# Layers run in halves of the tokens, per-token sums as single columns, x loaded first

## The chip, the cores and the metric

One core of a Trainium2 chip runs the whole program in one launch. The time is the device time of that launch in microseconds (us). Before the change it is 2333.32 us, the median of 3 runs (2330.7 to 2334.06). The profiled execution took 2335.25 us; its records cover a span of 2333.5 us. Engines are named as in the profile: PE is the matrix engine (PEld its loads of the stationary operand), DVE the vector engine, ACT the scalar engine, POOL GpSimd, SP the engine that issues most loads. An operand written 128x1024 has 128 partitions and 1024 elements in each.

## What is computed

`x` is 1024 tokens by 1024 features, float32. First come two layers of this form (`l` = 0, 1):

```python
shift, scale, gate = jnp.split(c_act @ w_ada[l] + b_ada[l], 3, axis=-1)
h = rms_norm(x, g_pre[l]) * (1.0 + scale) + shift
proj = h @ w_in[l]                       # 1024 -> 3072
y_a = b_a * causal_conv(c_a * u_a) * silu(gate_a)
y_p = causal_pool(u_p, ...) * silu(gate_p)
y = concatenate([y_a, y_p]) @ w_out[l]   # 1024 -> 1024
x = x + gate * rms_norm(y, g_post[l])
```

Then one hybrid layer:

```python
h = x @ w_in_2          # gmlp, two attentions, an index projection
mix = concatenate([gmlp(...), diff_attention(...), topk_attention(...)])
x = layer_norm(alpha * x + mix @ w_out_2, ln1_g, ln1_b)
gate, up = split(x @ w_gu_2)             # 2 x 2816
x = layer_norm(alpha * x + (silu(gate) * up) @ w_down_2, ln2_g, ln2_b)
```

Every norm needs, for each token, a sum over all 1024 features of its row. So the next product cannot begin for a token before the last product has ended for that token; for other tokens it could.

## The kernel before

**Layout.** Features lie on the partitions, in KT = 8 blocks `k` of 128, and the 1024 tokens lie along the free axis, as two halves of 512. A bank pair in PSUM (`bank[0..3]`, the name `pair` in the trace) holds 128 features of all 1024 tokens. A product of one *unit* makes one such block of 128 output features from all 1024 input features. Each float32 operand is split in two parts, `w_hi`/`w_lo` and `act_hi`/`act_lo`, and for each `k` three products are summed (hi·hi, hi·lo, lo·hi), each for both halves: 8 x 3 x 2 = 48 matmuls of 128x512 for a unit (`product`, L1565).

**Weights.** Units follow each other in two slots. For each unit SP loads 512 KB into `w_raw` (L446), ACT rounds it to `w_hi` (`hi_next`, L674), DVE makes `w_lo` (`lo_next`, L1022), and PE uses both. `w_hi` of a unit waits until PE has done with the unit two before it (`unit_done`), and the load waits for `lo_ready` of the unit before it in its slot.

**Order.** No scheduler is at work: each engine runs its instructions in the written order, and semaphores with constant or loop-counted values make it wait. What stands behind a waiting instruction in a queue waits too.

**Start.** SP loads the small parameters, then all of `x` as one transfer of 4 MB, then 16 pieces of `w_ada` (scale and shift of layer 0) four at a time. PE turns `x` into `xT` (L1487), DVE copies (L948) and sums the pieces weighted by `c` (L956, L958), `columns` (L1501) adds them over the partitions by matmuls against one column of ones.

**Per-token sums.** The squares of `x` or `y` (ACT L641, L720) are summed over the 8 blocks, for `y` on POOL (L573, L576), and over the partitions by `feature_sums` (L1494): a matmul with the square 128x128 `ones` as the stationary operand and 512 tokens moving, so that every partition gets all sums. DVE picks the diagonal (L965), reduces it to a column `rstd_col` (L967), scales and inverts it (L968, L969), ACT takes the root (L649), DVE makes a diagonal matrix of it (L973) and PE spreads it over the partitions again (L1508).

**A layer's end.** When all 8 units of the out projection are done, DVE scales `yT` (L1121) and adds it to `xT` for even `k` (L1127), POOL adds it for odd `k` (L581). Layer 1 then needs the sums of squares of the new `x`, and scales it: DVE L1032, ACT `act_hi` L683, DVE `act_lo` L1036. `product_two` (L1543, L1551) runs the first two units together, the parts with `act_hi` first, as they become ready `k` by `k`.

**The hybrid layer.** `act_hi` (L734) of the new `x`, two index units and one smaller, then 8 chunks of the value product (L1647) with 20 rounds of index scores (L1667 on PE, L764 on ACT, L1161/L1163 on DVE) between their steps, one every 3 steps; unit 0 and 1, 8 more chunks (L1647 again), units 2 to 13 (L1683), beside which the top-k threshold is found bit by bit; then attention in 48 items (L1735, L1749, L1767). Its output is scaled (L1387), turned (L1806) and multiplied by `w_out_2` (8 units, sum `z` L1398). The layer norm has a mean by matmul (L1820, L1827), centring (L1407), squares (ACT L888, POOL L625), their sum (L1494), root and spread as above, the scaling (L1416), `act_lo` (L1425) and the start of the second sum (L1431). The FFN's 22 hidden blocks go in groups of 6, 6, 6 and 4: gate and up units, `f_buf` (L1442), `f_hi` (L906), `f_lo` (L1444), then 8 units of the down product with partial sums on DVE (L1451). A second layer norm ends it: ACT shift (L919), PE turns (L1861), copies (L924, L1471), stores.

## Time and profile before

| what | value |
| --- | --- |
| median of 3 runs | 2333.32 us |
| profiled execution, its own time | 2335.25 us |
| span of its records | 2333.5 us |
| PE busy | 2168.3 us, 93% |
| DVE busy | 1038.1 us, 44% |
| ACT busy | 723.7 us, 31% |
| POOL busy | 168.8 us, 7% |
| mean granted clock of PE | 0.961 |

A share of busy time is an average. PE is near full for most of the span and has its idle time at a few places: the start, the two ends of layers, the way out of attention, the two layer norms. The rows that show them stand two sections below. The mean granted clock is 1 at PE's full rate and 0.5 at its lower one.

### The profile page before, as it was taken

How to read it: one execution, taken by the hardware profiler on the slowest of the kernel's cores; microseconds unless marked ns; L12 is line 12 of the kernel's file. 1: busy time of each engine (PE TensorE's matmuls, PEld its weight loads, DVE VectorE, ACT ScalarE, POOL GpSimd, SP SyncE). 2: the span in 40 equal slices, each digit the busy share in tenths (PEclk: the TensorE clock that was granted, in tenths of full speed). 3: DMA queues.
4: the chain of work that ended last, by engine and by line, in shares of the span. 5: the costliest groups of instructions: out<-in, count | busy, mean ns of one | idle time of the engine just before them, and what ended most of it. 6: DMA issues, size and time to landing. Idle time of an engine off the chain costs nothing.

```text
span 2333.5 us, 25535 instructions
## 1 busy us (share of the span) xinstructions
PE 2168.3 (93%) x9718; PEld 1698.4 (73%) x9718; DVE 1038.1 (44%) x1521; ACT 723.7 (31%) x1042; POOL 168.8 (7%) x132
## 2 busy tenths in 40 slices
PE   4899999889999988999988998979999999999995
PEld 3688887568888756688855667748888888888872
DVE  5744452453233235867778862262222222222235
ACT  2222123232212334555765552133211111111114
POOL 0000001200000121021200000210000000000021
PEclk9899999899999989999979999979999999999997
DMA  6423331101111104101100002101111112112101
GB/s 230 127 88 116 100 99 45 36 23 50 45 45 45 46 18 147 46 20 28 55 28 1 1 1 91 46 8 54 45 54 46 48 41 59 49 40 59 36 27 72
DMA packets 177131, 129.37 MB, mean 55 GB/s; under 512 B 5653, under 2 KB 167590, under 8 KB 176806
## 3 DMA queue, kind: packets, MB, share of 16 engines
q1 hardware_dynamic: 172454, 111.67, 15.6%
q0 software_dynamic: 4608, 16.78, 2.1%
q8 instruction: 44, 0.72, 0.1%
q14 instruction: 25, 0.20, 0.0%
HBM read 120.04 MB, written 8.39 MB: 55 GB/s over the span
## 4 chain that ended last, share of the span: by engine, by line
PE 83%; DVE 9%; ACT 4%; issue 1%; DMA 1%; POOL 0%; SPq 0%; DVEq 0%; ACTq 0%; PEldq 0%
PE pair L1565 59%; PE pair L1543 5%; PE pair L1683 4%; PE pair L1647 4%; PE pair L1767 2%; PE pair L1551 2%; PE pair L1735 1%; PE pair L1494 1%; DVE act_region L1310 1%; PE pair L1749 1%; DVE yT L1121 1%; PE pair L1667 1%; PE pair L1508 1%; ACT proj L785 1%; DVE xT L1127 1%
## 5 line engine op out<-in xcount | busy, mean ns | idle before, releaser
L1022 DVE TENSOR_TENSOR w_lo<-w_raw,w_hi 128x1024 fp32r<-128x1024 f32 x147 | 180.2, 1226 | 995.5 <-ACT w_hi L674 995.4
L1565 PE MATMUL pair<-act_hi,w_hi 128*128 128x512 f32 x1680 | 518.3, 390 | 4.0 <-DVE w_lo L1022 2.4
L1565 PE MATMUL pair<-act_lo,w_hi 128*128 128x512 f32 x1680 | 517.3, 389 | 0.0
L1565 PE MATMUL pair<-act_hi,w_lo 128*128 128x512 f32 x1680 | 517.2, 389 | 0.0
L674 ACT ACTIVATE w_hi<-w_raw 128x1024 fp32r<-128x1024 f32 x148 | 157.0, 1061 | 1010.2 <-PE pair L1565 954.3
L1565 PEld LDWEIGHTS pair<-act_hi,w_hi 128*128 128x128 f32 x1680 | 314.4, 188 | 73.1 <-issue 8.5
L1565 PEld LDWEIGHTS pair<-act_lo,w_hi 128*128 128x128 f32 x1680 | 315.3, 188 | 65.7
L1565 PEld LDWEIGHTS pair<-act_hi,w_lo 128*128 128x128 f32 x1680 | 315.3, 188 | 65.5
L1565 PE MATMUL pair<-f_hi,w_hi 128*128 128x512 f32 x352 | 108.5, 389 | 2.2 <-DVE f_lo L1444 2.2
L1565 PE MATMUL pair<-f_lo,w_hi 128*128 128x512 f32 x352 | 108.4, 389 | 0.0
L1565 PE MATMUL pair<-f_hi,w_lo 128*128 128x512 f32 x352 | 108.4, 389 | 0.0
L1543 PE MATMUL pair<-act_hi,w_hi 128*128 128x512 f32 x224 | 78.4, 434 | 24.6 <-ACT act_hi L734 10.4
L1767 PEld LDWEIGHTS pair<-proj,act_region 128*128 128x128 f32 x576 | 73.8, 202 | 34.5 <-issue 18.7
L1767 PE MATMUL pair<-proj,act_region 128*128 128x128 f32 (+1 forms) x576 | 82.7, 292 | 2.1 <-ACT act_region L845 2.1
L1735 PE MATMUL pair<-proj 64*128 64x512 f32 (+3 forms) x288 | 72.0, 582 | 8.9 <-DVE neg_max L1310 5.8
L835 ACT ACTIVATE act_region<-act_region,neg_max 128x128 f32<-128x128 f32 (+7 forms) x96 | 73.4, 768 | 16.9 <-DVE neg_max L1310 16.7
L1565 PEld LDWEIGHTS pair<-f_hi,w_hi 128*128 128x128 f32 x352 | 66.0, 188 | 16.2 <-issue 2.6
L1543 PEld LDWEIGHTS pair<-act_hi,w_hi 128*128 128x128 f32 x224 | 44.3, 209 | 44.4 <-issue 18.0
L1565 PEld LDWEIGHTS pair<-f_hi,w_lo 128*128 128x128 f32 x352 | 66.1, 188 | 13.7
L1565 PEld LDWEIGHTS pair<-f_lo,w_hi 128*128 128x128 f32 x352 | 66.1, 188 | 13.7
L1543 PE MATMUL pair<-act_hi,w_lo 128*128 128x512 f32 x224 | 75.7, 422 | 0.0
L615 POOL COPY sum<-z 128x1024 f32<-128x1024 f32 x2 | 2.1, 1039 | 962.6 <-DVE z L1451 704.5
(306 smaller groups left out, 2706.5 us busy)
## 6 DMA issues: line engine op xcount, KB each, us to landing
w_raw<-w_in SPq DMA_DIRECT2D x64, 512.0 KB, 3.8
w_raw<-w_gu SPq DMA_DIRECT2D x44, 512.0 KB, 3.8
w_raw<-w_out SPq DMA_DIRECT2D x24, 512.0 KB, 4.1
w_raw<-w_down SPq DMA_DIRECT2D x24, 384.0 KB, 3.4
sq<-w_ada POOLq DMA_DIRECT2D x16, 512.0 KB, 3.6
sq_sum<-w_ada POOLq DMA_DIRECT2D x16, 512.0 KB, 4.6
yT<-x SPq DMA_DIRECT2D x1, 4096.0 KB, 14.5
x_mid<-xT SPq DMA_DIRECT2D x1, 4096.0 KB, 18.7
```

The lines of the kernel that those rows point to most:

```text
L674: A(w_hi[s_][:], w_raw[s_][:], ACT.Copy).then_inc(hi_ready, 1)
L785: A(sign_out[i], score[:, sel_at(i):sel_at(i) + keys(i)], ACT.Sign, bias=f32(cand[:, q:q + 1]), accum_out=cnt[:, q:q + 1]).then_inc(signs_ ...
L835: A(prob[item % 3][m][:, 0:n], prob[item % 3][m][:, 0:n], ACT.Exp, scale=-1.0, bias=neg_max[:, item % 3, m, n > HALF:(n > HALF) + 1], accu ...
L1022: v.tensor_tensor(w_lo[s_][:], w_raw[s_][:], f32(w_hi[s_][:]), ALU.subtract)\
L1121: i = v.scalar_tensor_tensor(yT[:, k, :], yT[:, k, :], post_gain[:, l, k:k + 1], bank[2][:], ALU.mult, ALU.mult)
L1543: mm(bank[r][:, h * HALF:(h + 1) * HALF], w[slot][:, k, :], act_hi[:, k, h * HALF:(h + 1) * HALF], start=(k == order[0] and w is w_hi), st ...
L1551: i = mm(bank[r][:, h * HALF:(h + 1) * HALF], w_hi[slot][:, k, :], act_lo[:, k, h * HALF:(h + 1) * HALF], start=False, stop=(k == order[-1]))
L1565: i = mm(bank[pair][:, h * HALF:(h + 1) * HALF], w[slot][:, k, :], a[:, k, h * HALF:(h + 1) * HALF], start=(k == 0 and w is w_hi and a is ...
L1647: i_ = mm(o, x_[:, k, t * P:(t + 1) * P], w[:, k, :], start=(k == 0 and c_ == 0), stop=(k == KT - 1 and c_ == 2))
L1683: i_ = mm(bank[pair][:, h * HALF:(h + 1) * HALF], w[u % 2][:, k, :], a[:, k, h * HALF:(h + 1) * HALF], start=(k == 0 and w is w_hi and a i ...
L1735: i_ = mm(bank[m][:, off:off + w], proj[at, q_, i * P:(i + 1) * P], proj[at, k_, a:a + w], start=not picked, stop=True)
L1767: i_ = mm(o, probT[g % 2][:, t * P:(t + 1) * P], w, start=(t == 0), stop=(t == i))
```

## The change

1. **Halves.** `half_product` makes one unit for one half of the tokens (24 matmuls of 128x512). It is used for the first four input units of each layer, all eight out-projection units of each layer, all eight of `w_out_2`, the first four FFN units, and the eight down units of the last group. Each of these 44 units is loaded, rounded and split twice, once for each half: 88 half products where 44 products were.
2. **Sums as columns.** `token_cols` takes a 128x128 tile of the squares as the stationary operand and one column of ones as the moving one: 4 matmuls of one column for a half. The result is a column for each token block, which DVE reads directly (L965 and L967 have no counterpart). `spread` is for one half.
3. **POOL** adds the squares in halves, those of `y` and, at the end of layer 0, those of `x` for half 0; `x_stat_late` sums half 1 of `x` on PE.
4. **Start.** `x` comes first, in 8 transfers; squares of the natural-layout `x` are summed by ACT; the scale pieces are summed by DVE, the shift by 64 one-column matmuls on PE; the small parameters go through ACT's queue.
5. **Hybrid layer.** Four value chunks run ahead of the index units, the index rounds are placed every 2.4 steps over the other four and unit 0.
6. **Attention's end.** The first half of the output is scaled inside attention and turned straight behind it, the second after two half products.
7. **FFN.** Groups of 4, 6, 6, 6; the layer norms are done by halves between products; the turns of half 0 of the output stand before the last two half products.

```diff
+SPLIT = 4
+P1_LOOP = P1_ROLES + SPLIT
+P1_UNITS = P1_ROLES * CB + SPLIT
-GROUPS = [min(FG, FB - g) for g in range(0, FB, FG)]
+GROUPS = [FB % FG] + [FG] * (FB // FG)
+ROUND_STEPS = 2.4
...
+            for t in range(TT):
+                sp.dma_start(yT[:, t, :], x[0, t * P:(t + 1) * P, :]).then_inc(x_tile[t], 16)
+            for t in range(KT):
+                sp.dma_start(act_region[:, t, :], w_ada_v[0, :, t, D:2 * D]).then_inc(scale_loaded[t], 16)
...
+            def x_sum(ks):
+                for k in ks:
+                    pool.wait_ge(xsq_ready, k + 1)
+                    if k == 0:
+                        pool.wait_ge(rstd_spread, 3)
+                        i = g.tensor_copy(sq_sum[:, half(0)], sqs[0][:, half(0)])
+                    else:
+                        pool.wait_ge(xsq_added, k)
+                        i = g.tensor_tensor(sq_sum[:, half(0)], sq_sum[:, half(0)], sqs[k % 2][:, half(0)], ALU.add)
+                    i.then_inc(xsq_added, 1)
...
+                y_sum(l, 0, range(KT - 1))
+                y_sum(l, 1, range(2))
+                x_odds(l, 0, (1, 3))
+                y_sum(l, 1, range(2, 3))
+                x_odds(l, 0, (5, 7))
+                if l == 0:
+                    x_sum(range(4))
+                y_sum(l, 1, range(3, 4))
+                if l == 0:
+                    x_sum(range(4, KT))
+                y_sum(l, 1, range(4, KT - 1))
+                x_odds(l, 1, range(1, KT, 2))
...
+            def token_cols(src, o, a, first, last):
+
+                for t in range(TT // 2):
+                    i_ = mm(o[:, a * HALF + t:a * HALF + t + 1], src[:, a * HALF + t * P:a * HALF + (t + 1) * P],
+                            ones[:, 0:1], start=first and t == 0, stop=last and t == TT // 2 - 1)
+                return i_
...
+            for t in range(KT):
+                pe.wait_ge(shift_loaded[t], 16)
+                for k in range(KT):
+                    i = mm(shift_cols[:, k:k + 1], act_region[:, KT + t, k * P:(k + 1) * P], c_col[:, t:t + 1],
+                           start=t == 0 and k == 0, stop=t == KT - 1 and k == KT - 1)
...
+                for d in range(KT):
+                    if d >= 2:
+                        pe.wait_ge(o_copied, (2 * l + 1) * KT + d - 1)
+                    chain_spread = None
+                    if d == 1:
+                        chain_spread = lambda: spread(0, 3 if l == 0 else 7)
+                    if l == 0 and d == 5:
+                        chain_spread = lambda: spread(0, 4)
+                    half_product(out0 + KT + d, d % 2, 1, (lambda k: split_at((4 * l + 3) * KT, k)) if d == 0 else None,
+                                 between=chain_spread)
+                    if d == 0:
+                        y_stat(l, 0, 1)
+                    if l == 0 and d == 4:
+                        pe.wait_ge(xsq_added, KT)
+                        token_cols(sq_sum, bank[3], 0, True, True).then_inc(stat_done, 1)
...
+            for a in range(2):
+                for d in range(KT):
+                    pe.wait_ge(acc_added, 2 + (len(GROUPS) - 1 + a) * KT + d - 1)
+                    half_product(U_LAST + a * KT + d, 2 + d % 2, a, f_split if a + d == 0 else None, range(GROUPS[-1]),
+                                 f_hi, f_lo, between=(lambda: ln_spread(1, 0)) if a and d == 4 else None)
+                    if a and d == 0:
+                        ln_mean(1, 0)
+                    if a and d == 3:
+                        ln_variance(1, 0)
+                    if a and d == 6:
+                        out_turn(range(TT))
+            ln_mean(1, 1)
+            ln_variance(1, 1, odd=True)
+            ln_spread(1, 1)
+            out_turn(range(TT, 2 * TT))
```

POOL at the end of layer 0, before the change: the squares of `y` are summed over all tokens (`sq_sum`, from the two buffers `sq` and `sq_odd`), then the odd blocks of `x` get their `y`.

```order
L573 COPY sq_sum<-sq 128x1024
L576 TENSOR_TENSOR sq_sum<-sq_sum,sq_odd 128x1024
L576 TENSOR_TENSOR sq_sum<-sq_sum,sq 128x1024
L576 TENSOR_TENSOR sq_sum<-sq_sum,sq_odd 128x1024
L576 TENSOR_TENSOR sq_sum<-sq_sum,sq 128x1024
L576 TENSOR_TENSOR sq_sum<-sq_sum,sq_odd 128x1024
L576 TENSOR_TENSOR sq_sum<-sq_sum,sq 128x1024
L581 TENSOR_TENSOR xT<-xT,yT 128x1024 x4
```

POOL at the same place after the change, from the first sum of half 1 on (L616 and L619 are `y_sum`, L625 `x_odds`, L632 and L635 `x_sum`):

```order
L616 COPY sq_sum<-sq 128x512
L619 TENSOR_TENSOR sq_sum<-sq_sum,sq_odd 128x512
L625 TENSOR_TENSOR xT<-xT,yT 128x512 x2
L619 TENSOR_TENSOR sq_sum<-sq_sum,sq 128x512
L625 TENSOR_TENSOR xT<-xT,yT 128x512 x2
L632 COPY sq_sum<-sq 128x512
L635 TENSOR_TENSOR sq_sum<-sq_sum,sq_odd 128x512
L635 TENSOR_TENSOR sq_sum<-sq_sum,sq 128x512
L635 TENSOR_TENSOR sq_sum<-sq_sum,sq_odd 128x512
L619 TENSOR_TENSOR sq_sum<-sq_sum,sq_odd 128x512
L635 TENSOR_TENSOR sq_sum<-sq_sum,sq 128x512
```

The odd additions to `x` and the new sum over `x` now stand between the sums of `y`'s second half, in one queue; four more adds of `x_sum` and `y_sum` in turn stand behind the last row.

PE at the end of layer 0, before the change: all sums stand behind the last unit of the out projection, and the next layer's first units (L1543) behind both spreads (L1508).

```order
L1494 MATMUL pair<-sq_sum,ones 128x512 x2
L1494 MATMUL pair<-sq_odd,ones 128x512 x2
L1508 MATMUL pair<-sq_sum,ones 128x512 x2
L1494 MATMUL pair<-sq,ones 128x512 x2
L1494 MATMUL pair<-sq_odd,ones 128x512 x2
```

PE after the change, in the second half of that out projection (L1932 is `half_product`, L1881 `token_cols`, L1888 `spread`): the sums of half 0 stand behind the first unit of half 1, and their spread in the middle of the second.

```order
L1932 MATMUL pair<-act_hi,w_lo 128x512
L1881 MATMUL pair<-ones,sq_sum 128x1 x4
L1881 MATMUL pair<-ones,sq_odd 128x1 x4
L1932 MATMUL pair<-act_hi,w_hi 128x512
L1932 MATMUL pair<-act_lo,w_hi 128x512
L1932 MATMUL pair<-act_hi,w_lo 128x512
L1932 MATMUL pair<-act_hi,w_hi 128x512
L1932 MATMUL pair<-act_lo,w_hi 128x512
L1932 MATMUL pair<-act_hi,w_lo 128x512
```

In place of four matmuls of 512 columns for all tokens stand eight of one column for half 0, and a product's matmuls stand on both sides of them.

## Rows read from the trace of the kernel before

**Rows 1.** Page, parts 1 and 4: busy time by engine; the last chain.

```profile
PE 2168.3 (93%) x9718; PEld 1698.4 (73%) x9718; DVE 1038.1 (44%) x1521; ACT 723.7 (31%) x1042; POOL 168.8 (7%) x132
...
PE 83%; DVE 9%; ACT 4%; issue 1%; DMA 1%; POOL 0%; SPq 0%; DVEq 0%; ACTq 0%; PEldq 0%
```

**Rows 2.** Chain of waits, 205 to 340 us: start us, length us, what.

```profile
210.68 1.68 PE pair L1501 x16
212.35 65.41 PE pair L1565 x288
```

**Rows 3.** Stretches: length; PE, PEld, DVE, ACT, POOL busy; clock; DMA share; GB/s.

```profile
0.00:96.40 96.40, 59.02 (x231) 41.36 (x231) 58.09 (x59) 27.81 (x29) 6.25 (x40) 0.86 0.49 171
49.60:76.90 27.30, 13.02 (x33) 8.67 (x34) 20.71 (x23) 9.48 (x11) 1.33 (x2) 0.50 0.65 209
...
439.10:509.00 69.90, 52.10 (x145) 29.31 (x143) 47.59 (x42) 26.09 (x28) 9.40 (x4) 0.83 0.03 8
...
849.00:917.90 68.90, 50.92 (x183) 34.46 (x181) 40.42 (x36) 26.95 (x26) 12.88 (x6) 0.82 0.33 117
917.90:1187.30 269.40, 265.61 (x1270) 206.27 (x1267) 200.11 (x424) 165.12 (x327) 45.42 (x19) 0.99 0.14 38
1411.20:1447.00 35.80, 29.87 (x132) 24.95 (x131) 13.02 (x12) 5.98 (x7) 0.19 (x1) 0.86 0.29 118
1512.50:1575.60 63.10, 45.80 (x130) 26.48 (x128) 41.41 (x41) 23.71 (x24) 7.04 (x3) 0.78 0.03 9
2274.60:2333.50 58.90, 30.15 (x97) 17.33 (x95) 29.81 (x35) 24.29 (x31) 7.04 (x3) 0.77 0.18 71
```

**Rows 4.** Chain of waits, 1000 to 1060 us: value chunks, a new stationary operand each matmul.

```profile
1004.21 43.52 PE pair L1647 x192
```

**Rows 5.** Page, part 5: a unit's weights, w_lo on DVE and w_hi on ACT.

```profile
L1022 DVE TENSOR_TENSOR w_lo<-w_raw,w_hi 128x1024 fp32r<-128x1024 f32 x147 | 180.2, 1226 | 995.5 <-ACT w_hi L674 995.4
...
L674 ACT ACTIVATE w_hi<-w_raw 128x1024 fp32r<-128x1024 f32 x148 | 157.0, 1061 | 1010.2 <-PE pair L1565 954.3
```

**Rows 6.** Page, part 6: loads of a unit, KB each, us to landing.

```profile
w_raw<-w_in SPq DMA_DIRECT2D x64, 512.0 KB, 3.8
```

**Rows 7.** Chain of waits at the start.

```profile
6.80 14.54 DMA yT<-x
...
21.39 4.95 PE pair L1487 x24
...
63.21 3.59 PE pair L1501 x16
```

**Rows 8.** Groups of instructions, shapes apart, whole span: busy, mean ns of one.

```profile
L581 POOL TENSOR_TENSOR xT<-xT,yT 128x1024 f32<-128x1024 f32 x8 | 18.9, 2358 | 58.0 <-DVE yT L1121 58.0
...
L1163 DVE SCALAR_TENSOR_TENSOR score<-buf_b,index_w,score 128x512 f32<-128x512 f32 x24 | 18.1, 752 | 0.9
L674 ACT ACT_TABLE_LOAD x14 | 18.0, 1283 | 142.4 <-PE pair L1565 104.3 <-PE pair L1551 38.1
```

**Rows 9.** Groups, 455 to 472 us: DVE adds beside POOL adds.

```profile
L1127 DVE TENSOR_TENSOR xT<-xT,yT 128x1024 f32<-128x1024 f32 x3 | 6.9, 2288 | 0.1
```

**Rows 10.** Chain of waits, 436 to 512 us: the first add on DVE, POOL idle.

```profile
452.32 1.23 DVE xT L1127
```

**Rows 11.** DMA, 880 to 925 us: the store of x_mid and loads beside it.

```profile
x_mid<-xT SPq DMA_DIRECT2D x1, 4096.0 KB, 18.7
...
w_raw<-w_in SPq DMA_DIRECT2D x4, 512.0 KB, 5.1
```

**Rows 12.** Chain of waits, 2226 to 2334 us.

```profile
2232.33 1.07 ACT f_hi L906
...
2234.91 39.72 PE pair L1565 x174
2274.64 1.72 PE pair L1820 x4
...
2310.63 5.39 PE pair L1861 x24
```

More of the change, by code:

```diff
@@ L57 @@
 FG = 6
-GROUPS = [min(FG, FB - g) for g in range(0, FB, FG)]
+GROUPS = [FB % FG] + [FG] * (FB // FG)
+F_AT = [sum(GROUPS[:g]) for g in range(len(GROUPS))]
 SEL0 = TOPK // P
@@ L927, in _ @@
+            ln_squares(1, 1, range(KT), odd=True)
+            ln_sqrt(1, 1)
+            shift(1, range(KT))
+            for n in range(TT, 2 * TT, 2):
+                leave(n)
         @block.vector
@@ L1473, in _ @@
+            ln_center(1, 1, range(KT))
+            ln_root(1, 1)
+            ln_scale(1, 1, range(KT))
+            for n in range(TT + 1, 2 * TT, 2):
+                dve.wait_ge(outT_done, n + 1)
+                v.tensor_copy(staged(n // 2)[:, half(1)], out_bank(n)).then_inc(out_copied_dve, 1)
         @block.tensor
```

1553 lines of the change are left out of this document (962 added, 591 removed).

## Prediction, made before the change was run

> **What bounds the kernel now.** I read the page first. PE is busy 2168 of 2333.5 us and makes up 83% of the chain that ended last [rows 1]: no other engine's work can be worth much unless PE waits for it. So the change can pay only where PE waits. The chain inside a dense stretch shows 288 product matmuls in 65.41 us, 0.2271 us each, so a unit of 48 costs 10.90 us and half a unit 5.45 [rows 2]. Then I cut the span at the places where the chain leaves the products, and took from each stretch [rows 3] the products that it holds, at that rate:
>
> - start, 96.4 us with 2 units (21.8): 74.6 lost
> - layer 0 to layer 1, 69.9 with 2 units: 48.1
> - layer 1 to the value chunks, 68.9 with 3 units (32.7): 36.2
> - attention to the out projection, 35.8 with 2 units: 14.0
> - first layer norm, 63.1 with 2 units: 41.3
> - last layer norm to the end: 58.9
>
> That is 273 us of loss, and the stock that the change draws on. The clock in these stretches is 0.77 to 0.86, in the index stretch 0.99: waiting also costs rate afterwards.
>
> **The matmuls themselves.** No product work is saved. Half products load a new stationary operand for each matmul instead of each second. The value chunks already do: 192 matmuls in 43.52 us, 0.2267 us each [rows 4]. I take 0; the two rows bound it between -0.2% and 0.
>
> **The weight queue.** 44 more units go through SP, ACT and DVE. A slot needs, per two half products (10.9 us), a load of 3.8 us [rows 6], 1.06 for w_hi and 1.23 for w_lo [rows 5], with some 0.4 of hand-over: 6.5 us. PE's 10.9 us hides it with 4.4 to spare, where before it had 15.3. I take 0. If loads land later than about 8.1 us the cover is gone, and each further us costs 0.5 us per half product.
>
> **Start.** Before, x came in one transfer of 14.5 us behind the parameters, and the turns took until 30 us [rows 7]. Now tiles are turned as they land. I walk: last tile at about 15, copies end 19, root and parameters 23.4, eight scale adds at 1.3 to 33, columns to 37, the scaling of half 0 on DVE 8 x 0.75 [rows 8], then low parts and half 1, to 52. The shift needs 64 one-column matmuls; a float32 matmul is two passes in the trace (8 columns are x16), so 128 passes. 16 passes took 3.59 us at the lower clock [rows 7] and 1.68 at the full one [rows 2]: 28.7 or 13.4 us, from about 37. In this stretch before, the clock was 0.50 for 27 us [rows 3]. By the first the products start at 67.6, by the second at 56.7. The first product then runs at the pace of DVE's halves (1.5 us per k), so the loss is 71.6 or 57.3: gain 3 to 17. I take 3, since thin PE work had the low clock there. Parameters late on ACT's queue could cost as much as 5 below nothing.
>
> **Layer 0 to 1.** Half 0's sums, root, spread and scaling now run beside half 1's products. Prices on PE: token_cols 8 passes of 0.105, 0.84 us [rows 2]; spread of one half two passes of 512 columns, 0.86 (four took 1.72 [rows 12]). POOL's half adds I price at half of 2.36 [rows 8], 1.2. Counted from the start of half 1 of the out projection: y sums 1.7 (twice 0.84), spread 0.9; y_normed on DVE (yT scaled and the even x added, in halves of 0.75) to 26; POOL works off, in one queue, the odd adds to x, then seven x_sum and one y_sum in turn: 28 + 8 x 1.22 = 38. PE has finished its fifth half product (d=4) at 30 and waits for xsq_added: 8.3 us. Then columns 0.8, spread 0.9, wait for the first scaled blocks of layer 1 1.8, y sums 1.7, spread 0.9, x_stat_late 7 (eight times 0.84), the wait for half 1's root 2 (ACT has a rounding of weights ahead of it), spread 0.9, and the first half product on half 1 follows DVE's pairs of scaling and low part, 1.5 us for each k: 14.2 with its start in place of 5.5, 8.7. Sum 35.5, and 3 for the clock after waits: 38.6 against 48.1, gain 9.5. Bounds: 0 if the waits on half 0's chain come whole, 30 if POOL, the root and the pacing are all hidden. This is the term I trust least, and the POOL wait is its core.
>
> **Layer 1 to the value chunks.** No x_sum here. Sums and spreads 1.7 + 0.9 + 1.7 + 0.9 + 1.5 of clock, and the index head (small unit's copies and turns, as before) 8: 14.6 against 36.2, gain 21.6 (14 to 30).
>
> **Index rounds and attention.** Rounds now come every 2.4 steps. DVE needs for one round 4 operations of 0.75 us [rows 8], 3.0; PE offers 2.9. DVE was busy 200 of 269 us in this stretch [rows 3]. So I take 2 us lost. In attention ob_scale (2.3) on DVE and two table loads of 1.28 [rows 8]: 3 lost. Together -5 (-12 to +2).
>
> **Attention's end.** Half 0 is scaled already, so its 16 turns (0.225 us each by 24 in 5.39 [rows 12]) follow at once: 3.6, copy 0.6, low part 0.7 and hand-overs, products 6.3 us after attention's end. Half 1's 16 turns behind the second half product cost 3.7. Loss 10 against 14: gain 4; 0 if half 1's scaling, 4 blocks on DVE behind the low parts, is late, 8 if both turns overlap.
>
> **First layer norm.** From the start of out projection half 1: mean 1.7 (four matmuls of 512 took 1.72 [rows 12]; here each half needs four passes, too), columns 0.8, spread 0.9, mean, wait 0.4, columns 0.8, spread of half 1 late by 3.5, because x1_start and the low parts of half 0 stand ahead of ln_root in DVE's queue, and the last half product paced by DVE, 6.1. With 2 for the clock 19 against 41.3: gain 22.3 (12 to 34).
>
> **FFN groups.** Before each down product the last f_hi and f_lo must come [rows 12]. The cover is smaller in a group of 4 and at the last group, where the product is a half: -3.3 (-6 to 0).
>
> **The end.** Half 1's chain stays whole but for half the width: last add 0.7, mean 0.9, centring 5.5, columns, root, spread, scaling 6, turns 6.6 in place of 5.4 plus 3.6 [rows 12], copy, store 4. On top half 0's mean, columns, spread and eight turns lie between products. I get 77.4 us from the start of the last eight half products, of 18 matmuls each, 32.7 us of work: 44.7 against 58.9, gain 14.2 (6 if half 0's turns find their blocks late, 24 if the last chain runs at full clock).
>
> **Sum.** 3 + 9.5 + 21.6 - 5 + 4 + 22.3 - 3.3 + 14.2 = 66.3. Span 2333.5 - 66.3 = 2267.2; the profiled run has 1.75 around its span, and stands 1.9 above the median, so the median should be 2267. The bounds, if not all on one side, give some 25 either way.
>
> A rule of the Trainium skill speaks against the change. First the row: beside POOL's adds a DVE add of two SBUF operands takes 2.29 us [rows 9], alone 1.23 [rows 10]. "GPSIMD Engine Reference", section Specifications, says that POOL's SBUF interfaces are shared with the vector engine, with contention for vector instructions that have two SBUF inputs; the trace agrees. The change gives POOL more adds, in smaller pieces, beside DVE's w_lo and x adds.
>
> **Rivals.**
>
> A. *More is hidden.* PE keeps its full clock through the short gaps and the shift runs at it (+14), POOL's sum comes in time (+8): 2245. For it: outside the start no wait of PE is forecast above 9 us, and the clock was 0.99 where work was thin but steady [rows 3]. Against: one-column matmuls kept the clock at 0.50 at the start for 27 us [rows 3, 7].
>
> B. *New waits in the queues.* Each boundary now threads ACT, DVE and POOL work for two halves between weight work in one written order. If every DVE add beside POOL costs 1.06 us more (2.29 - 1.23) for some 8 adds at each of two layer ends, 17 us, and both layer norms wait 6 more: 2296. For it: rows 9. Against: only the waits at the end of a half reach PE.
>
> C. *Slower.* The weight queue becomes the bound. Its place is the slot: load, w_hi, w_lo, per two half products. Loads at 9.7 us would cost 0.8 us in each of 88 half products, 70 us: 2337. It decides from 8.1 us of landing. Against: loads took 3.8, and 5.1 even beside a 4 MB store [rows 11]; DMA is idle for most of the span.
>
> D. *Nothing moves*, because gains and new waits cancel: needs all low bounds at once.
>
> **Numbers.** Forecast 0.52 (2253 to 2282), A 0.18, B 0.22, C 0.06, D 0.02. The range 2238 to 2296 leaves out C, D, and the outer parts of A and B. What a measurement of this kernel can tell from no change is about 0.2%, 4.7 us: faster 0.92, same 0.02, slower 0.06.
>
> **What would show it.** The first half product near 67 us (57 if A); PE waiting some 8 us for POOL's x sum in the fifth half product of half 1 in layer 0, in layer 1 nothing like it; token_cols 0.8 us per four at full clock; a last half product with gaps at each k after layer 0; the spread of half 1 late by 3 to 4 us in the first layer norm; down products waiting 2 to 3 us for f_lo; the last 45 us of the span without products. A product rate above 0.2271 us per matmul in the half products, or PE waiting for w_lo again and again, would make the forecast wrong; so would gaps that sum to much over 210 us.

## The result, and the profile after

The changed kernel takes 2294.89 us (median of 4, 2294.0 to 2295.67), the one before 2333.69 beside it: the ratio is 0.9834, with a 95% interval of 0.9817 to 0.9851. It is 39 us faster. The prediction had 2267 in a range of 2238 to 2296: the direction held, the range held by 1 us at its slow end, and more than a third of the forecast gain did not come. The span of the profiled execution is 2292.2 us, 41.3 less than before, where 66.3 were forecast.

The page of the changed kernel, parts 1 and 4, against [rows 1]:

```profile
PE 2168.5 (95%) x9910; PEld 1737.5 (76%) x9910; DVE 1093.6 (48%) x1702; ACT 752.1 (33%) x1191; POOL 225.6 (10%) x194
...
PE 81%; DVE 8%; ACT 5%; issue 2%; POOL 2%; DMA 1%; ACTq 0%; DVEq 0%; SPq 0%; POOLq 0%
```

PE is busy for as long as before, and the span is shorter by its idle time. Busy is not full rate: the mean granted clock is 0.956, where it was 0.961. POOL, with 0% of the chain before, has 2%: the first sign of a new wait.

For the account I cut both traces where they have done the same product work: at the start of layer 0's out projection, the first dense loop of layer 1, the second row of value chunks, the dense products behind attention and behind the first layer norm, and the last eight half products. The two other cuts are the first index round and attention's last product; where the product work before a cut differs, it is taken off at 0.2271 us a matmul.

| stretch | forecast gain, us | measured gain, us |
| --- | --- | --- |
| start | 3 | 6.3 |
| layer 0 to 1 | 9.5 | 0.6 |
| layer 1 to the index rounds | 21.6 | 12.4 |
| index rounds | -2 | -7.9 |
| attention | -3 | -1.9 |
| attention's end | 4 | 4.8 |
| first layer norm | 22.3 | 21.9 |
| FFN groups, to the last eight half products | -3.3 | -6.4 |
| from there to the end | 14.2 | 11.5 |

The last column sums to 41.3, as the spans differ. The ends of the two layers miss 18.1 us, the rounds 5.9, the FFN groups 3.1, the end 2.7; the start gave 3.3 more than forecast.

At the start the chain of waits of the changed kernel reads as follows, with [rows 7]:

```profile
32.89 3.57 PE pair L1875 x16
36.46 27.32 PE pair L1900 x128
...
65.73 4.45 PE pair L1932 x11
```

The shift's 128 passes took 27.3 us, and the first half product starts at 65.7 (67.6 was forecast). Three stretches of the changed kernel, with the columns of [rows 3]:

```profile
36.50:63.70 27.20, 27.20 (x128) 27.18 (x128) 13.23 (x20) 0.00 (x0) 0.00 (x0) 0.50 0.39 135
472.80:486.00 13.20, 13.07 (x77) 11.84 (x76) 4.23 (x6) 4.62 (x7) 2.54 (x2) 0.73 0.21 60
419.90:438.40 18.50, 7.23 (x23) 5.75 (x23) 5.42 (x5) 7.47 (x13) 13.15 (x9) 0.63 0.20 58
```

The first of the three is those passes: PE counts as busy for all of the 27.2 us, and its granted clock is 0.50, the lower level of 1.2 GHz. The second is in layer 1, where PE was hardly idle either and the clock is 0.73. The third holds a wait of PE for POOL. Its chain, at the end of layer 0:

```profile
428.88 1.27 POOL sq_sum L635
...
430.30 1.27 POOL sq_sum L635
431.57 0.04 issue
431.61 1.86 PE pair L1881 x8
433.48 5.01 PE pair L1932 x12
438.48 0.86 PE pair L1888 x2
```

PE had nothing to do from 420.3 to 431.6; in the list of its waits:

```profile
PE pair L1881 <- POOL sq_sum L635: 11.3, 1, 11.3
```

Then four columns took 1.86 us, and 12 product matmuls 5.01, where full clock gives 0.84 and 2.72. The bunches of one-column matmuls in layer 1 (`x_stat_late`) stand in the same chain:

```profile
472.80 4.12 PE pair L1881 x32
476.92 5.33 PE pair L1932 x12
482.25 3.63 PE pair L1881 x32
```

Behind a bunch of 4.1 us with no idle time, 12 matmuls again took twice their time. And at the end of layer 1 there is a wait that the prediction did not have:

```profile
827.44 0.63 SPq L485
828.08 0.05 issue
828.12 0.02 SPq L453
828.14 0.03 issue
828.17 9.55 DMA w_raw<-w_out
...
837.81 1.06 ACT w_hi L740
...
838.89 1.24 DVE w_lo L1241
```

L485 is the store of half 0 of `x_mid`. It stands in SP's queue ahead of two loads of `w_out`, and waits for POOL's last odd addition. The load behind it took 9.55 us beside the 2 MB store, and PE stood still for 7.2 us.

In the FFN, the down products of the first and of the last group start behind a wait of PE for `f_lo` (2.2 and 2.9 us):

```profile
1611.24 28.84 PE pair L1916 x119
...
2181.07 35.22 PE pair L1932 x147
```

At 0.2271 us a matmul these are 27.0 and 33.4 us: 1.8 us more in each, and the granted clock is 0.71 from 1611.2 to 1617 and 0.72 from 2181 to 2187.

### The profile page after: what moved, and what is told of

Its sections match the earlier page's. It is cut to its first block, busy times and chain, and to the rows that moved or that the text cites. A ratio compares the mean times of both kernels' runs of the same rounds, so it can differ in the third digit from the quotient of the medians.

```text
span 2292.2 us, 26136 instructions
## 1 busy us (share of the span) xinstructions
PE 2168.5 (95%) x9910; PEld 1737.5 (76%) x9910; DVE 1093.6 (48%) x1702; ACT 752.1 (33%) x1191; POOL 225.6 (10%) x194
## 4 chain that ended last, share of the span: by engine, by line
PE 81%; DVE 8%; ACT 5%; issue 2%; POOL 2%; DMA 1%; ACTq 0%; DVEq 0%; SPq 0%; POOLq 0%
PE pair L1916 47%; PE pair L1932 16%; PE pair L2088 4%; PE pair L2056 3%; PE pair L2189 2%; PE pair L2157 2%; PE pair L1900 1%; DVE act_region L1596 1%; PE pair L2171 1%; PE pair L2076 1%; DVE w_lo L1241 1%; POOL sum L692 1%; ACT proj L934 1%; PE pair L1881 1%; ACT w_hi L740 1%
## 5 line engine op out<-in xcount | busy, mean ns | idle before, releaser
L1247 DVE TENSOR_TENSOR w_lo<-w_raw,w_hi 128x1024 fp32r<-128x1024 f32 x101 | 123.8, 1226 | 687.0 <-ACT w_hi L747 687.0
L1916 PE MATMUL pair<-act_hi,w_hi 128*128 128x512 f32 x1328 | 409.5, 390 | 3.9 <-ACT v_all L875 1.8
L1916 PE MATMUL pair<-act_lo,w_hi 128*128 128x512 f32 x1328 | 408.9, 389 | 0.0
L1916 PE MATMUL pair<-act_hi,w_lo 128*128 128x512 f32 x1328 | 408.9, 389 | 0.0
L747 ACT ACTIVATE w_hi<-w_raw 128x1024 fp32r<-128x1024 f32 x102 | 108.2, 1061 | 824.8 <-PE pair L1916 824.8
L1916 PEld LDWEIGHTS pair<-act_hi,w_lo 128*128 128x128 f32 x1328 | 249.3, 188 | 51.9
L1916 PEld LDWEIGHTS pair<-act_lo,w_hi 128*128 128x128 f32 x1328 | 249.2, 188 | 51.8
L1932 PE MATMUL pair<-act_hi,w_hi 128*128 128x512 f32 x576 | 238.9, 415 | 21.6 <-DVE w_lo L1241 7.2
L1241 DVE TENSOR_TENSOR w_lo<-w_raw,w_hi 128x1024 fp32r<-128x1024 f32 x92 | 121.6, 1322 | 240.4 <-ACT w_hi L740 240.2
L1932 PE MATMUL pair<-act_lo,w_hi 128*128 128x512 f32 x576 | 232.2, 403 | 0.0
L1932 PE MATMUL pair<-act_hi,w_lo 128*128 128x512 f32 x576 | 231.6, 402 | 0.0
L740 ACT ACTIVATE w_hi<-w_raw 128x1024 fp32r<-128x1024 f32 x90 | 95.0, 1058 | 281.6 <-PE pair L1932 230.7
L1932 PEld LDWEIGHTS pair<-act_hi,w_hi 128*128 128x128 f32 x576 | 112.9, 196 | 55.7 <-issue 19.2
L1932 PEld LDWEIGHTS pair<-act_hi,w_lo 128*128 128x128 f32 x576 | 112.9, 196 | 24.8
L1932 PEld LDWEIGHTS pair<-act_lo,w_hi 128*128 128x128 f32 x576 | 113.4, 197 | 24.0 <-issue 1.9
L2189 PEld LDWEIGHTS pair<-v_all,act_region 128*128 128x128 f32 x576 | 73.4, 201 | 35.0 <-ACT act_region L996 17.9
L2189 PE MATMUL pair<-v_all,act_region 128*128 128x128 f32 (+1 forms) x576 | 82.6, 292 | 2.7 <-ACT act_region L996 2.7
L1916 PE MATMUL pair<-f_hi,w_hi 128*128 128x512 f32 x256 | 79.3, 391 | 2.2 <-DVE f_lo L1788 2.2
```

The source lines that it names most:

```text
L740: A(w_hi[u % 2][:], w_raw[u % 2][:], ACT.Copy).then_inc(hi_ready, 1)
L747: A(w_hi[s_][:], w_raw[s_][:], ACT.Copy).then_inc(hi_ready, 1)
L1241: v.tensor_tensor(w_lo[u % 2][:], w_raw[u % 2][:], f32(w_hi[u % 2][:]), ALU.subtract)\
L1247: v.tensor_tensor(w_lo[s_][:], w_raw[s_][:], f32(w_hi[s_][:]), ALU.subtract)\
L1916: i = mm(bank[pair][:, h * HALF:(h + 1) * HALF], w[slot][:, k, :], a[:, k, h * HALF:(h + 1) * HALF], start=(k == 0 and w is w_hi and a is ...
L1932: i_ = mm(o, w[u % 2][:, k, :], x_[:, k, half(a)], start=(k == order[0] and w is w_hi and x_ is hi), stop=(k == order[-1] and w is w_lo))
```

## The experiments

All are edits of the changed kernel. The first four ran on one chip, the next four on a second, three on a third, one of them the changed kernel itself, and the last on a fourth; each time is set against runs of the kernel before on the same chip. 0.9834 (second time 0.9828, below) is the ratio of the changed kernel; its interval is 0.9817 to 0.9851, so steps of a few us are told apart by the traces and not by the times. Seven profiled executions of kernels whose code from the first to the second out projection is the changed kernel's took 407.4 to 409.1 us there; that is the scatter against which that stretch is read.

**The store behind the loads.**

```diff
                 for n in range(KT + 1, 2 * KT):
                     load_out(l, n)
-                    if l == LAYERS - 1 and n == KT + 5:
-                        sp.wait_ge(x_even, KT // 2 * (2 * l + 1))
-                        sp.wait_ge(x_odd, KT // 2 * (2 * l + 1))
-                        sp.dma_start(x_mid[:, :, half(0)], xT[:, :, half(0)]).then_inc(x_kept, 16)
+                if l == LAYERS - 1:
+                    sp.wait_ge(x_even, KT // 2 * (2 * l + 1))
+                    sp.wait_ge(x_odd, KT // 2 * (2 * l + 1))
+                    sp.dma_start(x_mid[:, :, half(0)], xT[:, :, half(0)]).then_inc(x_kept, 16)
```

> Edit to the changed kernel: the store of the first half of x_mid (2 MB) is issued behind the last w_out load of layer 1 instead of between the loads of units 13 and 14. Theory 1 (the load of a w_out unit stands in SP's queue behind the wait for x and behind the store, and PE's gap of 7.58 us at 832.7 us is that load, which took 9.55 us to land): the gap goes, the load lands in about 4 us, and the time falls by 6 to 8 us to about 2288. Rival (the gap belongs to POOL's adds to x and the roots, which end at 827 us, and the load only came last): a gap of 4 us or more stays near there and the time falls by less than 3 us.

Measured: 2286.58 us, ratio 0.9802 (0.9789 to 0.9815). From the start of the second out projection to the index units the trace has 118.3 us instead of 125.6, 7.3 less, and the chain holds products without a wait:

```profile
809.90 24.52 PE pair L1932 x108
834.42 0.14 issue
834.55 11.13 PE pair L1932 x48
```

The gain is 7 us by the ratios too, as theory 1 had it: the wait was the load's place in the queue. The first row also gives the rate of half products, 0.2270 us each.

**Columns apart.**

```diff
-                                 between=((lambda: spread(1, 5)) if q == 1 else
-                                          (lambda: x_stat_late(range(4, KT))) if q == 3 else None))
+                                 between=(lambda: spread(1, 5)) if q == 1 else None,
+                                 each=((lambda k: x_stat_late([k - 4]) if k >= 4 else None) if q == 2 else
+                                       (lambda k: x_stat_late([k + 4]) if k < 4 else None) if q == 3 else None))
                     if q == 0:
                         y_stat(0, 1, 3)
-                    if q == 2:
-                        x_stat_late(range(4))
```

(`each` is called behind the three matmuls of a step `k`.)

> Edit: the one-column matmuls that sum the squares of half 1 of x in layer 1 (x_stat_late, 8 times four tiles) stand one k at a time between the steps of two half products, instead of in two bunches of 32 passes (4.1 and 3.6 us). The same matmuls, as many. Theory 1 (a bunch of one-column matmuls lets the clock fall, and the 12 product matmuls behind each took 5.33 and 4.47 us where 2.73 is the full rate): no such slow stretch, granted clock near 1 between 470 and 490 us, time down by 3 to 4 us to about 2291. Rival (what is slow there is PE waiting for squares from ACT): the columns' waits move between the steps and the time stays within 1.5 us of 2294.9.

Measured: 2291.79 us, ratio 0.9825 (0.9812 to 0.9839). The intervals of this and of the unedited kernel overlap, so the time alone does not decide. In the trace, from the first to the second out projection it has 404.8 us where the changed kernel has 408.9, 4.0 less and below all seven unedited executions. The stretch behind, to the index units, has 1.7 more (as it has in two executions that are unedited in both stretches), so 2.3 us are left there. The same stretch of time reads

```profile
472.80:486.00 13.20, 12.97 (x89) 11.58 (x88) 6.50 (x10) 4.63 (x7) 3.79 (x3) 1.00 0.27 79
...
474.76 0.79 PE pair L1881 x8
475.54 0.80 PE pair L1932 x3
476.34 0.79 PE pair L1881 x8
```

The same one-column matmuls, with three product matmuls between each four columns, stood at a clock of 1.00 instead of 0.73 in this execution. PE was as busy in both. This agrees with theory 1, but one execution does not show it: in three of the four later kernels with this edit the clock fell among the same columns (last section).

**Half 0's sum on PE.** `x_sum` is taken out of POOL's queue, and for half 0 of layer 0:

```diff
+            def x_stat_first(k):
+                pe.wait_ge(xsq_ready, k + 1)
+                token_cols(sqs[k % 2], bank[3], 0, k == 0, k == KT - 1).then_inc(sq_taken, 1)
...
-                                 between=chain_spread)
+                                 between=chain_spread, each=x_stat_first if l == 0 and d == 4 else None)
                     if d == 0:
                         y_stat(l, 0, 1)
-                    if l == 0 and d == 4:
-                        pe.wait_ge(xsq_added, KT)
-                        token_cols(sq_sum, bank[3], 0, True, True).then_inc(stat_done, 1)
```

> Edit: the sum of the squares of half 0 of x at the end of layer 0 is made by PE columns, one k behind each step of the fifth half product (8 times 0.84 us), instead of by eight adds on POOL (x_sum) and one set of columns. Theory 1 (PE's 11.7 us at 420 us are POOL's serial adds of 1.28 us, and the clock falls in that wait, 12 matmuls in 5.01 us): PE pays 6 us of columns and loses neither the 11.7 us wait nor the slow matmuls; time down by 6 to 9 us to about 2287. Rival (the odd x adds on POOL and the squares on ACT are as late, so PE waits for xsq_ready instead): a wait of over 4 us stays in the fifth half product and the gain is under 4 us.

Measured: 2290.98 us, ratio 0.9817 (0.9804 to 0.983): some 4 us less, not the 6 to 9 of theory 1, and the interval overlaps the unedited kernel's. The trace has 403.1 us from the first to the second out projection, 5.7 less than 408.9, and 2.1 more in the stretch behind. PE waits nowhere for the squares (steps of 0.79 and 0.79 us), and pays 6.3 us of columns, so the wait did belong to POOL's sum. The next half product comes behind a wait for ACT, whose queue the squares had held, and its 12 matmuls took 4.56 us: part of the gain stays there. (In the kernel with the shared index keys the same 12 took 2.99 us.)

```profile
425.50 0.79 PE pair L1876 x8
426.28 0.81 PE pair L1927 x3
427.09 0.02 issue
427.12 1.07 ACT w_hi L735
428.18 4.56 PE pair L1927 x12
```

**The shift on DVE.**

```diff
-            for t in range(KT):
-                pe.wait_ge(shift_loaded[t], 16)
-                for k in range(KT):
-                    i = mm(shift_cols[:, k:k + 1], act_region[:, KT + t, k * P:(k + 1) * P], c_col[:, t:t + 1],
-                           start=t == 0 and k == 0, stop=t == KT - 1 and k == KT - 1)
-            i.then_inc(ada_col, 1)
+            pe.wait_ge(shift_used, KT)
+            columns(gate_buf, shift_cols).then_inc(ada_col, 1)
...
+            for t in range(KT):
+                dve.wait_ge(shift_loaded[t], 16)
+                ada_add(gate_buf, act_region[:, KT + t, :], t, shift_used)
+                dve.wait_ge(shift_used, t + 1)
```

(DVE's queue is also put in another order behind this: the low parts of half 0 come ahead of the scaling of half 1.)

> Edit: the shift of layer 0 is summed by DVE (8 operations of 1.29 us behind the scale's) and put into columns by 8 one-column matmuls, instead of 64 one-column matmuls on PE (128 passes in 27.3 us). Theory 1 (these passes run at the lower clock, 0.213 us each, and the first half product waits for nothing else): products start at about 52 us instead of 65.7, time down by 10 to 14 us to about 2283. Rival (the pieces of w_ada land too late, or DVE's own queue of scaling and low parts becomes the chain): products start after 58 us and the gain is under 6 us.

Measured: 2281.82 us, ratio 0.9781 (0.9767 to 0.9794), the largest single step. The first half product starts at 53.20 us instead of 65.73. What bounds the start now is the landing of the shift's pieces and DVE behind them:

```profile
27.35 11.26 DMA act_region<-w_ada
...
43.98 1.30 DVE gate_buf L1208
...
53.20 27.01 PE pair L1933 x110
```

**Rounds over 64 steps.**

```diff
-ROUND_STEPS = 2.4
+ROUND_STEPS = 3
...
-            unit(0, 3, rounds_in(4) + [(s_ + KT, n) for s_, n in rounds_in(5)])
+            pe.wait_ge(vc_copied, TT)
+            unit(0, 0, rounds_in(4) + [(s_ + KT, n) for s_, n in rounds_in(5)])
+            unit(1, 3, rounds_in(6) + [(s_ + KT, n) for s_, n in rounds_in(7)])
             pe.wait_ge(relu_done, 4 * len(ROUNDS))
-            unit(1, 1)
+            pe.wait_ge(p3_copied, 1)
```

(On ACT, the rounding of the second value weights goes between the last rounds.)

> Edit: an index round every 3 steps instead of every 2.4, over four value chunks, unit 0 and unit 1 (64 steps instead of 48). Unit 0 is made in bank pair 0 and unit 1 in pair 3, so that unit 1 does not wait for the rounds' banks, and ACT's rounding of the second value weights goes between the last rounds. Theory 1 (packed into four chunks and one unit, the rounds are bound by ACT and DVE, about 2.9 us for each, and PE waits in them and 2 us behind them): the stretch from the first round to the second row of value chunks shrinks from 72.5 us by 4 to 8 us, time 2287 to 2290. Rival (each round costs PE the same wherever it stands, since PE waits for the relu of the round before): the stretch stays within 2 us of 72.5, or grows by the wait for unit 0's exit from pair 0.

Measured: 2303.11 us, ratio 0.986 (0.9843 to 0.9878), 9 us more span than the changed kernel; the intervals just touch. Theory 1 fell: the stretch did not shrink but grew by 2.4 us, a little more than the rival allowed. This does not show that distance is worth nothing, since ACT's roundings of 1.94 us came between the rounds with the same edit, and the chain of this kernel runs through DVE's scores at the last two rounds. And a loss of 7.5 us came that neither theory had: from the second row of value chunks to attention the trace has 190.8 us instead of 183.3. The bit search of the top-k starts behind the last round, and at 1013.1 PE waits 4.2 us for ACT, which does the search's signs ahead of a chunk's exit.

**Variance columns later.**

```diff
-                                 f_hi, f_lo, between=(lambda: ln_spread(1, 0)) if a and d == 4 else None)
+                                 f_hi, f_lo, between=(lambda: ln_spread(1, 0)) if a and d == 5 else None)
...
-                    if a and d == 3:
+                    if a and d == 4:
                         ln_variance(1, 0)
```

> Edit: in the last down group the variance columns of half 0 stand behind the fifth instead of the fourth half product, and the spread in the sixth. Theory 1 (PE's wait of 2.9 us at 2231 us is POOL's serial sum of squares, and the 12 matmuls behind it in 4.96 us are at the lower clock): both go, minus 4 to 5 us, about 2290. Rival (the scaling and shift of half 0 are then too late for its turns, out_turn): PE waits before the turns for as much, and the time stays within 1.5 us of 2294.

Measured: 2299.14 us, ratio 0.9849 (0.9834 to 0.9865), not faster, and 4.7 us longer in span, 4.0 of them behind the start of the last eight half products. Theory 1 fell, and the rival had the kind of wait but not its place or size. Without the wait for POOL, PE waits 4.2 us at 2231.9 and 3.2 at 2247.9:

```profile
2232.11 1.05 ACT w_hi L740
...
2233.18 2.20 DVE w_lo L1241
2235.39 0.61 DVE z L1806
...
2236.04 5.97 PE pair L1932 x18
```

ACT's and DVE's work for the next half product had been hidden by the wait for POOL. DVE's `w_lo` took 2.20 us, with POOL adding all the while.

**Four edits together** (the first four of these).

> The four edits of the first experiments together (store behind the loads; columns of half 1 apart; sum of half 0 by PE columns; shift summed by DVE). Theory 1 (they lie at four different places and add up, as read from their traces 7.3 + 4.0 + 5.7 + 12.5): 2293.8 - 29.5 = 2264. Rival (a gain at one place is given back at the next boundary, because ACT and DVE are then the later ones): over 2272.

Measured: 2268.94 us, ratio 0.9713 (0.9695 to 0.9732). Against 0.9834 that is 28 us of the 29.5, nearer to theory 1's 2264 than to the rival's 2272; but the five runs lie between 2264.3 and 2273.8, two of them above 2272. The profiled execution is the slowest, and its span is 20.2 us below the changed kernel's: 12.1 at the start, 7.3 at the store, and only 4.1 from the first to the second out projection, where 9.7 were to come, with 3.3 lost elsewhere. In three later kernels with the same code that stretch gave 7.9, 8.1 and 12.7. So the places add up to within this scatter, and no closer.

**All six edits.**

> The four edits of the kernel before in this list, with the rounds over 64 steps and the later variance columns. By the theory that all places are apart: 2264 less 4 to 8 less 4 to 5, about 2254. By the rivals of the two added edits: as the kernel with four, 2264.

Measured: 2278.2 us, ratio 0.9762 (0.9742 to 0.9782): 9 us above the kernel with four, about what the two added edits had cost alone (6 and 4 by the ratios). Both expectations, 2254 and 2264, were missed.

**The changed kernel again**, on the third chip.

> The changed kernel itself, unedited, run beside the others on one chip, so that they are compared with it and not with a run on another chip. Expected: ratio to before 0.983 as when it was first timed; all theories agree.

Measured: 2295.3 us, ratio 0.9828 (0.9814 to 0.9842).

**DVE's additions over half the columns** in the rounds.

```diff
-                        x_ = v.scalar_tensor_tensor(sc, r, index_w[:, i, h:h + 1], sc, ALU.mult, ALU.add)
+                        x_ = v.scalar_tensor_tensor(sc[:, 0:w // 2], r[:, 0:w // 2], index_w[:, i, h:h + 1],
+                                                    sc[:, 0:w // 2], ALU.mult, ALU.add)
```

The kernel leaves out half of these multiply-adds, so its index scores are incomplete; it serves only to take DVE's work away.

> Edit to the changed kernel: in the index rounds DVE's multiply-adds (7 of 8 heads) cover only the left half of each piece's columns, so the index scores are not those of the reference; ACT's relus and all waits stay. Theory 1 (packed every 2.4 steps, the rounds are bound by DVE, 4 operations of 0.75 us each a round): the stretch from the first round to the second row of value chunks shrinks from 72.5 us by 4 us or more, and the start of attention moves forward by at least that. Rival (PE's wait in each round is for ACT's relu of the round before, whatever DVE does): the stretch stays within 1.5 us of 72.5.

Measured: 2295.61 us, against 2295.3 on the same chip, and the stretch is 72.6 us against 72.5. The rival held. DVE does not bound the rounds of the changed kernel; it waits 23.5 us in them for ACT, where it waited 9:

```profile
ACT buf_a L909 <- PE pair L2077: 23.8, 19, 2.5
...
DVE score L1450 <- ACT buf_a L909: 12.1, 10, 2.0
DVE score L1448 <- ACT buf_a L909: 11.4, 9, 2.4
```

**Index keys shared**: the four edits, and

```diff
-            for g in range(4):
+            for g in (0, 3):
                 A(proj[32 * g:32 * g + 32, S_IK, :], bank[2][0:32, :], ACT.Copy).then_inc(ik_copied, 1)
...
+            dve.wait_ge(ik_copied, 2)
+            for g in (1, 2):
+                v.tensor_copy(proj[32 * g:32 * g + 32, S_IK, :], proj[0:32, S_IK, :]).then_inc(ik_copied, 1)
```

> The kernel with four edits (store behind the loads, columns apart, sum by PE, shift by DVE), and two of ACT's four copies of the index keys (1.01 us each, PE idle for 4.15 us beside them) made by DVE from the first copy. Theory: ACT's chain is two copies shorter, DVE's copies run beside it, PE's gap falls from 4.15 to about 2.5 us, and the time is 1.5 to 2 us below the kernel with four edits. Rival: DVE is late there (it still makes the low parts of half 1 and w_lo), the gap stays. Against the unedited changed kernel on the same chip: 0.987 or less.

Measured: 2263.61 us, ratio 0.9693 (0.9672 to 0.9715), and 0.986 of the changed kernel beside it; against the four edits alone (0.9713) the intervals overlap. In the list of waits PE's gap fell from 3.8 to 2.1 us, as the theory had it, DVE's two copies taking 0.68 and 0.69.

**Rounds by their width**, on top of that.

```diff
+STEPS_AFTER = {P: 1, 2 * P: 1, 3 * P: 2, 4 * P: 3}
+ROUND_AT = [sum(STEPS_AFTER[r[2]] for r in ROUNDS[:n]) for n in range(len(ROUNDS))]
...
-    return [(s_ % KT, n) for n in range(len(ROUNDS)) for s_ in [int(ROUND_STEPS * n) + 1] if s_ // KT == part]
+    return [(s_ % KT, n) for n, s_ in enumerate(ROUND_AT) if s_ // KT == part]
```

> The kernel with the shared index keys (four edits and two copies on DVE), and the index rounds placed by their width: 3 steps behind a piece of 512 columns, 2 behind 384, 1 behind 256 and 128, in 45 steps from the start of the fifth value chunk. Theory 1 (what PE waits for in a round is ACT's four relus of the round before, 0.60 us each at 512 columns, whatever DVE does; two steps of products, 1.58 us with their entry, are too short behind them, three are enough): rounds behind 512 columns take 1.07 us and none 1.4 or more, the stretch from the first round to the second row of value chunks (72.5 us in the changed kernel) shrinks by 2 to 4 us. Rival (the last wait of 2.1 us and the slow matmuls behind it are all of it): the stretch stays within 1 us.

Measured: 2261.57 us, ratio 0.968 (0.9661 to 0.9699), not told from the kernel before it by the times. In the trace the part from the first round to attention is 254.1 us against 256.9 in that kernel, 2.7 less, and the stretch of the expectation is 2.8 us shorter than in that kernel and 3.5 shorter than in the changed one. The rounds behind 3 steps took 1.07 to 1.11 us:

```profile
916.72 2.26 PE pair L2066 x9
918.98 1.07 PE pair L2086 x8
920.05 2.26 PE pair L2066 x9
...
941.49 1.65 PE pair L2086 x7
```

A round behind fewer steps took up to 1.65, where theory 1 had none of 1.4 or more; the rest of it stands. At one round (910 to 914 us) the chain runs through four of DVE's scores, so DVE is not far behind ACT. This is the fastest kernel of the study, 2262 us, 1.5% below the changed one by the ratios.

## Why the prediction was right or wrong

**What bounds the kernel, and the stock.** Right: busy time of PE stayed (2168.5), and the gain is idle time. Of the 273 us some 230 are left.

**The matmuls themselves.** Right: half products run at 0.2270 us a matmul, with a new stationary operand for each.

**The weight queue.** Right: loads landed in 3.8, 3.9 and 3.1 us by kind, and nothing points to a bound there. Rival C fell, with one exception that has another cause: the one load at 828 us, late through its place in SP's queue and a store beside it. The prediction looked at landing times in general, and not at what stands in front of each load. "Each queue that it is moved past" would have found it: the store of half 0 moved from behind the loads to between them, with its wait.

**Start.** Right in the choice of the lower clock, with 65.7 us for 67.6. That choice was partly luck: the row that it leaned on, 49.6 to 76.9 us of [rows 3], has PE busy for only 13.0 of 27.3 us, so its clock of 0.50 could not tell what one-column passes do; only the 3.59 us of [rows 7] could. The gain was 6.3 instead of 3, since the pacing behind the start, priced at 4 us, took about 2. (The fast branch does not add up: 56.7 with the same 4 us is 60.7, not 57.3; this touches only the upper bound and rival A.) That the passes hold the start is read from the chain, where nothing stands between them and the shift's addition, and borne out by the shift on DVE, which brought 12.5 us.

**Layer 0 to 1.** The term was mis-sized most: 0.6 for 9.5. The steps had the right order, and the wait for POOL came where forecast, but was 11.3 us instead of 8.3: POOL's `x_sum` began 0.7 us later, its adds took 1.27 us, not 1.2, with 0.1 between, and the one `y_sum` among them 2.2. The larger part is the clock, for which 3 us stood in the sum. The rows show 3.3 (four columns and 12 matmuls behind the wait), 2.6 and 1.8 (12 matmuls behind each bunch, 5.33 and 4.47 for 2.72), and 1.1 for the spread at 492.4 (1.98 for 0.86), 8.8 together. Wait and clock make 3.0 and 5.8 more than was forecast, which is what the row misses. How much of the part behind the bunches comes of their being bunches stays open: set apart, the same columns ran at 1.00 in two profiled executions and at the lower clock, for part of them, in three. Bringing the sum to PE gave 5.7 in this stretch.

**Layer 1 to the value chunks.** Of the missing 9.2 us, 7.3 are the load behind the store, shown by moving the store. Some 2 us are a wait of PE at 877.8 us, which the forecast left out: the chain goes from POOL's last odd addition over ACT's `act_hi` to ACT's exit of a value chunk (`v_all`) and to PE.

**Index rounds.** The loss was 7.9, not 2, and the step that named DVE is wrong: halving its work changed nothing. PE needs the relus of the round before, and ACT's four take 2.4 us at 512 columns; two steps of products (1.6 us) are too short behind them. From the end of the products before a round to the next products, the 20 rounds take 25.7 us in the changed kernel and 19.7 in the one before: 2.2 of the 6.0 more are the last round, for whose relus unit 1 waits, 3.8 the others. Behind that wait the clock falls (48 matmuls in 12.8 us for 10.9, 1.9 us). Placing the rounds by width gave 2.8 back, which shows the spacing's part; the rest is read from the trace. Before, three steps lay between any two rounds, and two more units behind. The loss came with the four value chunks that went ahead to cover half 1's chain. The price of attention, 1.9 for 3, was about right.

**Attention's end, first layer norm.** Right within 1 us each: 4.8 for 4, 21.9 for 22.3. At attention's end 16 turns took 1.75 us, 0.11 each, not 0.225, which was the price of turns at the end of the span.

**FFN groups.** 6.4 lost for 3.3. The waits for `f_lo` came where forecast, in the small first group (2.2 us) and at the last (2.9, against 2.2 before). What was left out is the clock behind each, 1.8 us twice; behind the one wait of the kernel before, the granted clock is 1.00 (174 matmuls in 39.72 us [rows 12]). No experiment was made here.

**The end.** 11.5 for 14.2. The wait for POOL's squares (2.5 us) was left out, and the clock: behind it 12 matmuls took 4.96 us, and in the last chain sets of four columns 1.88 instead of 0.84. Moving the columns later did not help, so the wait for POOL is one of two that end close together; what it would take to get the missing 2.7 us back is open.

**POOL beside DVE.** On the page of the changed kernel `w_lo` has a mean of 1226 ns in the loops (L1247) and 1322 in the parts written out (L1241): 81 of those 92 took 1.23 us, and 11, each with POOL at work for part of its time or all of it, 1.65 to 2.31. The half adds to `xT` (L1280) have a mean of 1111 ns, and took 0.69 us where POOL was idle. By the Trainium skill's rule ("GPSIMD Engine Reference", Specifications: contention with vector instructions that have two SBUF inputs) this was to be expected, and the trace agrees. On the path this counted little: in the last group PE waits 0.85 us behind a `w_lo` of 2.23. Rival B's mechanism was right, its price by this route too high.

**The rivals.** A's bet on the clock fell at the start (0.50 with PE busy) and at each layer's end. B came nearest in size, 2296 for 2295, and that is luck: in place of the slow DVE adds that it priced stand a load behind a store, a longer wait for POOL, ACT's relus and the clock behind each wait. The forecast itself, 2253 to 2282 with a chance of 0.52, missed: most of its list of waits was right, and the terms that were mis-sized are the clock after waits (3 us in layer 0 to 1 for 8.8, nothing in the rounds, the FFN and the last group) and the rounds. Beside them stand waits that were not on the list, the load behind the store above all.

## What to carry to other kernels

When work is cut in halves to hide a chain, list for each queue what now stands between two loads or two units: a wait that was harmless at the end of a queue stops the stream in its middle. A long run of one-column matmuls filled PE's time here at the lower clock, so make such a sum on another engine that has time (12.5 us at the start); setting them apart between product matmuls helped in some executions only. Price each new wait with the slow matmuls behind it: here 1.1 to 3.3 us behind each. Cover that is moved to one place is missing at another: before moving products ahead of a wait, see what they covered where they stood.

## What the runs showed of the hardware

- 128 passes of one column kept PE busy for 27.2 of 27.2 us at a granted clock of 0.50; with 64 such passes in two bunches a 13.2 us stretch had a clock of 0.73, and with the same passes in eights between three matmuls of 512 columns 1.00 in the profiled execution.
- A DVE subtraction of two SBUF operands, 128x1024, took 1.23 us alone and 2.20 with POOL adding all the while (e.g. at 2232.8 us of the changed kernel).
- The clock among columns that stand between product steps was not the same in every execution. In the kernel with the shared index keys, and in the one with the rounds by width, the same instructions run here (eight passes of one column, then three product matmuls, in turn):

```profile
457.90:464.00 6.10, 5.95 (x42) 5.52 (x43) 0.85 (x2) 1.73 (x3) 0.00 (x0) 1.00 0.31 89
...
459.00:467.00 8.00, 7.85 (x32) 7.12 (x31) 0.06 (x1) 0.63 (x1) 0.00 (x0) 0.50 0.23 66
```

The first row is of the kernel with the shared keys. With PE busy for all but 0.15 us in either, one ran at 1.00 and the other at 0.50. Both have the same short delay of PE just before, some 0.25 us for ACT's square (at 457.9 and 457.2 us); in the second the clock fell 1 to 2 us behind it, as in the kernels with four and with six edits, and in the first it did not. From the first out projection to the second the four profiled executions of this same code took 396.2, 400.8, 401.0 and 404.8 us. This can be where the scatter of these kernels comes from: 2256.6 to 2268.7 us in five runs of one, against 2294.0 to 2296.2 for the changed kernel on the same chip. The runs behind the scatter have no trace, so that is not shown. The Trainium skill ("TensorE: Matmul & The Clock Gate", What's actually happening) says that the clock follows how busy PE has been, and that where it changes differs from run to run. The second half agrees with these rows; the first they do not decide, since the busy time of the profile was full in each of them.
